# Making the S5 tables during the up projection of the MLP ahead, with the first quarter's fills in its down projection, and silu written to PSUM

## The reference

```
for i in range(DEPTH):
    h = rms_norm(x, norm_mix[i])
    y = [dsa_mixer, rwkv7_mixer, s5_mixer][i % 3](h, ...)
    x = x + y
    x = x + conv_ffn(rms_norm(x, norm_ffn[i]), ...)

def conv_ffn(h, w_up, conv_w, conv_b, w_down):
    u = h @ w_up                        # 1024 -> 2 * 2816
    u = causal_conv_3(u) + conv_b       # one filter of 3 taps per channel
    gate, val = split(u, 2)
    return (silu(gate) * val) @ w_down  # 2816 -> 1024

def s5_mixer(h, a_re, a_im, log_step, b_re, b_im, c_re, c_im, ...):
    step = exp(log_step)
    lam = a_re + 1j * a_im
    lam_bar = exp(lam * step)
    b_bar = (lam_bar - 1) / lam * b
    # 64 groups of 16 channels, state of 64 complex numbers each:
    # state = lam_bar * state + b_bar u ;  y = real(c state) + d h ; gelu ; GLU
```

## Time and profile before

| | |
|---|---|
| median of three runs | 1615.17 us |
| profiled execution, whole | 1617.21 us |
| its span, first to last instruction | 1615.5 us |
| PE busy | 1480.8 us, 92% |
| DVE busy | 1032.3 us, 64% |
| ACT busy | 749.6 us, 46% |
| POOL busy | 618.9 us, 38% |
| chain that ended last | PE 74%, DVE 18%, ACT 4%, issue 2%, POOL 1% |

### The profile page before, as it was taken

One profiled execution on the slowest core, in us unless ns is written; L12 is line 12 of the kernel. 1 busy time (PEld: TensorE's weight loads), 2 busy tenths in 40 slices (PEclk: granted clock), 3 DMA queues, 4 the chain that ended last, 5 costly groups with the idle time before them and its releaser, 6 DMA issues.

```text
span 1615.5 us, 33199 instructions
## 1 busy us (share of the span) xinstructions
PE 1480.8 (92%) x14000; PEld 1382.5 (86%) x14000; DVE 1032.3 (64%) x1572; ACT 749.6 (46%) x1186; POOL 618.9 (38%) x300
## 2 busy tenths in 40 slices
PE   7989999999998884999998546999999998999998
PEld 7888999988787773999987546999999988999998
DVE  4695476735584458467688996467752498367752
ACT  4466465531342332365552212556554457456543
POOL 5322366740010010287652001446754232346763
PEclk9999999999999995999999778999999999999999
DMA  5533355552442001365553001545555343445553
GB/s 156 169 119 105 119 178 187 179 184 93 130 134 77 4 4 51 105 181 186 176 172 122 1 1 54 183 131 183 182 189 169 125 132 105 131 130 181 184 185 103
DMA packets 212054, 210.12 MB, mean 130 GB/s; under 512 B 12098, under 2 KB 211058, under 8 KB 211922
## 3 DMA queue, kind: packets, MB, share of 16 engines
q1 hardware_dynamic: 210784, 206.65, 39.8%
q0 software_dynamic: 800, 1.46, 0.5%
q10 hardware_dynamic: 338, 0.10, 0.0%
HBM read 207.15 MB, written 1.05 MB: 129 GB/s over the span
## 4 chain that ended last, share of the span: by engine, by line
PE 74%; DVE 18%; ACT 4%; issue 2%; POOL 1%; ACTq 0%; DMA 0%; DVEq 0%; POOLq 0%
PE psum L379 16%; PE psum L381 15%; PE psum L380 15%; PE psum L663 7%; PE psum L473 5%; DVE work L2225 4%; PE psum L665 3%; DVE w_low L362 3%; ACT w_high L354 2%; PE psum L410 1%; DVE work L1126 1%; PE psum L1492 1%; PE psum L1506 1%; PE psum L403 1%; DVE work L1931 1%
## 5 line engine op out<-in xcount | busy, mean ns | idle before, releaser
L362 POOL TENSOR_TENSOR w_low<-ring,w_high 128x1024 fp32r<-128x1024 f32 (+1 forms) x184 | 509.6, 2770 | 869.4 <-ACT w_high L354 825.0
L379 PE MATMUL psum<-x_high,w_high 128*128 128x256 f32 x2048 | 589.4, 288 | 28.2 <-issue 16.0
L380 PE MATMUL psum<-x_low,w_high 128*128 128x256 f32 x2048 | 583.6, 285 | 0.0
L381 PE MATMUL psum<-x_high,w_low 128*128 128x256 f32 x2048 | 583.5, 285 | 0.0
L354 ACT ACTIVATE w_high<-ring 128x1024 fp32r<-128x1024 f32 (+1 forms) x368 | 361.7, 1034 | 261.3 <-PE psum L381 159.9
L379 PEld LDWEIGHTS psum<-x_high,w_high 128*128 128x128 f32 x2048 | 397.0, 194 | 34.8 <-issue 20.5
L380 PEld LDWEIGHTS psum<-x_low,w_high 128*128 128x128 f32 x2048 | 397.3, 194 | 1.0 <-issue 1.0
L381 PEld LDWEIGHTS psum<-x_high,w_low 128*128 128x128 f32 x2048 | 397.2, 194 | 0.0
L362 DVE TENSOR_TENSOR w_low<-ring,w_high 128x1024 fp32r<-128x1024 f32 (+1 forms) x184 | 250.8, 1364 | 173.6 <-ACT w_high L354 173.1
L749 DVE SCALAR_TENSOR_TENSOR work<-psum,par,work 128x255 f32<-128x255 f32 (+1 forms) x352 | 145.5, 476 | 147.6 <-ACT work L688 147.5
L663 PE MATMUL psum<-inner,w_high 128*128 128x512 f32 x528 | 186.4, 398 | 2.6 <-DVE w_low L362 2.6
(11 more groups left out here) (303 smaller groups left out, 1874.6 us busy)
## 6 DMA issues: line engine op xcount, KB each, us to landing
ring<-in_ffn_w_up_dram SPq DMA_DIRECT2D x88, 1024.0 KB, 5.1
ring<-in_ffn_w_down_dram SPq DMA_DIRECT2D x32, 1024.0 KB, 5.0
ring<-in_dsa_w_in_dram SPq DMA_DIRECT2D x28, 1024.0 KB, 5.2
ring<-in_ffn_w_down_dram SPq DMA_DIRECT2D x16, 768.0 KB, 4.3
ring<-in_rwkv_w_rkv_dram SPq DMA_DIRECT2D x12, 1024.0 KB, 5.1
ring<-in_dsa_w_out_dram SPq DMA_DIRECT2D x8, 1024.0 KB, 5.1
ring<-in_s_w_glu_dram SPq DMA_DIRECT2D x8, 1024.0 KB, 5.7
ring<-in_rwkv_w_out_dram SPq DMA_DIRECT2D x4, 1024.0 KB, 5.1
```

Of the source, the lines that this page charges most:

```text
L362: eng.tensor_tensor(low, raw, high.bitcast(F32), ALU.subtract).then_inc(sem("w_split", b), 1)
L379: pe.matmul(out_, lhs[0], rhs[0], start=start, stop=False, skip_group_check=True)
L380: pe.matmul(out_, lhs[0], rhs[1], start=False, stop=False, skip_group_check=True)
L381: return pe.matmul(out_, lhs[1], rhs[0], start=False, stop=stop, skip_group_check=True)
```

## The change

- The S5 tables: in the MLP of layer 1, PE transposes `a` after pair 1 and `c` after pair 3. ACT does its two parts after pairs 4 and 5. DVE does table part 0 after pair 4, parts 1 and 2 after pair 6, 3 and 4 after pair 7, 5 and 6 after pair 8, 7 and 8 after pair 9, 9 and 10 after pair 10, and part 11 in step 0 of the down projection.
- The fills of quarter 0 (12 instructions of 1024 elements a row) are made in steps 1, 3, 5 and 7 of that down projection, three in each. `s5_dve` begins with quarter 1.
- The loop over the pairs is written out for this MLP.
- FB and GC are put in other slots of the work area, and the squares of the norm ahead of S5 go where `hT` will be.
- In all four MLPs, silu is written to the PSUM bank of the gate tile, and the product of gate and value reads it there. That bank is free for PE when the product is made, where before it was free when the taps were.

```diff
@@ over_up_tiles
+            if before_s5(L):
+                for j in range(UP_TILES // 2):
+                    pair(j, 0)
+                return
@@
+        TURN_A, TURN_C = 1, 3
+        TABLE_PARTS = {4: (0,), 6: (1, 2), 7: (3, 4), 8: (5, 6), 9: (7, 8), 10: (9, 10)}
+        STEP_PARTS = {0: (11,)}
+        EARLY_FILLS = (1, 3, 5, 7)
@@ freed
-                freed[(L, "up", 2 * j)] = (("taps_done", L), 4 * j + 2)
+                freed[(L, "up", 2 * j)] = (("gated_done", L), j + 1)
@@ add_down
-                        s5_tables(dve, 3 * m + g)
+                        for part in STEP_PARTS.get(3 * m + g, ()):
+                            s5_tables(dve, part)
+                        if 3 * m + g in EARLY_FILLS:
+                            s5_fill(dve, 0, EARLY_FILLS.index(3 * m + g))
@@ mlp_pe
-                if before_s5(L) and j == UP_TILES // 2 - 2:
+                if before_s5(L) and j == TURN_A:
                     s5_turn_a(pe)
-                if before_s5(L) and j == UP_TILES // 2 - 1:
+                if before_s5(L) and j == TURN_C:
                     s5_turn_c(pe)
@@ mlp_act
-                act.activation(conv[:, j % 3, 0], conv[:, j % 3, 0], ACT.Silu).then_inc(sem("silu_done"), 1)
+                act.activation(bank_of((L, "up", 2 * j))[:, :].rearrange("p (c t) -> p c t", c=2), conv[:, j % 3, 0],
+                               ACT.Silu).then_inc(sem("silu_done"), 1)
                 if j:
                     round_inner(j - 1, r)
+                if before_s5(L) and j in (TURN_C + 1, TURN_C + 2):
+                    s5_exponentials(act, j - TURN_C - 1)
@@ mlp_dve
-                dve.tensor_tensor(gated[:, j % 3], conv[:, j % 3, 0], conv[:, j % 3, 1],
-                                  ALU.mult).then_inc(sem("gated_done"), 1)
+                dve.tensor_tensor(gated[:, j % 3], bank_of((L, "up", 2 * j))[:, :].rearrange("p (c t) -> p c t", c=2),
+                                  conv[:, j % 3, 1], ALU.mult).then_inc(sem("gated_done"), 1)
+                if before_s5(L):
+                    for part in TABLE_PARTS.get(j, ()):
+                        s5_tables(dve, part)
@@ s5_fill (a quarter's FB is half 0 and 1, its GC half 2 and 3)
+            if part == 0:
+                step.mark(dve.tensor_tensor(out_, re, x, ALU.mult))
+                tt(t, im, y, ALU.mult)
+                tt(out_, out_, t, ALU.subtract)
+                return
+            tt(out_, re, y, ALU.mult)
+            tt(t, im, x, ALU.mult)
...
@@ s5_dve
-            for q in range(4):
-                fill(FB, b_raw, q, FB_RE, FB_IM, "fb_done")
-                if q:
-                    turned_in(q - 1)
-                    scan(q - 1)
-                    toeplitz(2 * q - 2)
-                    toeplitz(2 * q - 1)
-                fill(GC, c_raw, q, GC_RE, GC_IM, "gc_done")
+            for q in range(1, 4):
+                s5_fill(dve, q, 0)
+                s5_fill(dve, q, 1)
+                turned_in(q - 1)
+                scan(q - 1)
+                toeplitz(2 * q - 2)
+                toeplitz(2 * q - 1)
+                s5_fill(dve, q, 2)
+                s5_fill(dve, q, 3)
```

More of the change, by code:

```diff
@@ L270, in trunk, with squares_of @@
         sq = [slot_view(8, DC, T), slot_view(13, DC, T)]
+        def squares_of(n):
+            return hT if n % 2 == 0 and layers[n // 2] % 3 == 2 else sq[n % 2]
         def updates(L, ffn=0):
@@ L599, in trunk, with over_up_tiles @@
             "p (j c t) -> p j c t", j=3, c=2)
-        def over_up_tiles(eng, pair):
+        def over_up_tiles(eng, pair, L):
+            if before_s5(L):
+                for j in range(UP_TILES // 2):
+                    pair(j, 0)
+                return
             for j in range(ROUND // 2):
@@ L627, in pair @@
                         done, offset = signal(name)
-                        pe.wait_ge(done, r * (4 * PJ) + (value + offset))
+                        pe.wait_ge(done, r * (PJ if name[0] == "gated_done" else 4 * PJ) + (value + offset))
                     else:
@@ L640, in pair @@
                     mm.then_inc(sem("bank_full", bank), 1)
-                if before_s5(L) and j == UP_TILES // 2 - 2:
+                if before_s5(L) and j == TURN_A:
                     s5_turn_a(pe)
-                if before_s5(L) and j == UP_TILES // 2 - 1:
+                if before_s5(L) and j == TURN_C:
                     s5_turn_c(pe)
-            over_up_tiles(pe, pair)
+            over_up_tiles(pe, pair, L)
             for m in range(4):
@@ L721, in pair @@
                     s5_load(pool, L + 1, j)
-            over_up_tiles(pool, pair)
+            over_up_tiles(pool, pair, L)
             rest_of_inner(UP_TILES // 2 - 1, 0)
@@ L730, in pair @@
             def pair(j, r):
-                if before_s5(L) and j == UP_TILES // 2 - 1:
+                if before_s5(L) and j == TURN_A + 1:
                     dve.wait_ge(sem("params_turned"), 1)
@@ L1955, in trunk @@
         QG = S5_Q * GW
-        FB, GC = (flat[:, i * 8192:(i + 1) * 8192].rearrange("p (q r g z) -> p q r g z", q=4, r=2, z=GW) for i in (0, 1))
+        FB, GC = ([work[:, i, :].rearrange("p (r g z) -> p r g z", r=2, z=GW) for i in slots]
+                  for slots in ((7, 1, 2, 3), (8, 5, 6, 0)))
         TZ = FB
         h_tok = work[:, 9, :].rearrange("p (h g s c) -> p h g s c", h=2, s=S5_L, c=S5_C)
-        y_tok = work[:, 8, :].rearrange("p (h s g c) -> p h s g c", h=2, s=S5_L, c=S5_C)
+        y_tok = work[:, 4, :].rearrange("p (h s g c) -> p h s g c", h=2, s=S5_L, c=S5_C)
         u_all = work[:, 10, :].rearrange("p (q h g n) -> p q h g n", q=4, h=2, n=S5_N)
@@ L1968, in trunk @@
         fill_tmp = work[:, 14, 1024:2048]
-        with_cos, with_sin = (work[:, 8, i * 512:(i + 1) * 512].rearrange("p (r z) -> p r z", r=2) for i in (0, 1))
+        with_cos, with_sin = (work[:, 4, i * 512:(i + 1) * 512].rearrange("p (r z) -> p r z", r=2) for i in (0, 1))
         decay8 = work[:, 15, 0:1024].rearrange("p (q z) -> p q z", q=4)
@@ L2321, in s5_tables, with s5_fill @@
                 double(2 ** (part - 7))
+        def s5_fill(dve, q, half):
+            step = vector_step
+            then, tt, ts, complex_product = s5_math(dve)
+            kind, part = half // 2, half % 2
+            dst, raw, c_re, c_im, signal_ = ((FB, b_raw, FB_RE, FB_IM, "fb_done"), (GC, c_raw, GC_RE, GC_IM, "gc_done"))[kind]
+            g = slice(q * S5_Q, (q + 1) * S5_Q)
+            shape = [P, S5_Q, S5_L, S5_C]
+            re, im = (raw[:, v, g].unsqueeze(2).to_broadcast(shape) for v in (0, 1))
+            x, y = (coef[:, v, :, g].rearrange("p k g -> p g k").unsqueeze(3).to_broadcast(shape) for v in (c_re, c_im))
+            out_ = dst[q][:, part].rearrange("p g (k c) -> p g k c", k=S5_L)
+            t = fill_tmp.rearrange("p (g k c) -> p g k c", g=S5_Q, k=S5_L)
+            if q == 0 and part == 0:
+                dve.wait_ge(*((sem("s5_in", 2), 16 * S5_DMAS[2]), (sem("c_ready"), 2))[kind])
+            if part == 0:
[5 more added lines that the diff above has]
+            tt(t, im, x, ALU.mult)
+            if dst is GC:
+                ins = dve.scalar_tensor_tensor(out=out_, in0=out_, scalar=-1.0, in1=t, op0=ALU.mult, op1=ALU.subtract)
+            else:
+                ins = dve.tensor_tensor(out_, out_, t, ALU.add)
+            ins.then_inc(sem(signal_), 1)
+            dve.wait_ge(sem(signal_), q + 1)
         def s5_dve(dve, L):
@@ L2325, in s5_dve @@
             then, tt, ts, complex_product = s5_math(dve)
-            def fill(dst, raw, q, c_re, c_im, signal_):
-                g = slice(q * S5_Q, (q + 1) * S5_Q)
-                shape = [P, S5_Q, S5_L, S5_C]
-                re, im = (raw[:, v, g].unsqueeze(2).to_broadcast(shape) for v in (0, 1))
-                x, y = (coef[:, v, :, g].rearrange("p k g -> p g k").unsqueeze(3).to_broadcast(shape) for v in (c_re, c_im))
-                out_ = [dst[:, q, v].rearrange("p g (k c) -> p g k c", k=S5_L) for v in (0, 1)]
-                t = fill_tmp.rearrange("p (g k c) -> p g k c", g=S5_Q, k=S5_L)
-                step.mark(dve.tensor_tensor(out_[0], re, x, ALU.mult))
-                tt(t, im, y, ALU.mult)
-                step.mark(dve.tensor_tensor(out_[0], out_[0], t, ALU.subtract))
-                tt(out_[1], re, y, ALU.mult)
-                tt(t, im, x, ALU.mult)
-                if dst is GC:
-                    ins = dve.scalar_tensor_tensor(out=out_[1], in0=out_[1], scalar=-1.0, in1=t, op0=ALU.mult,
-                                                   op1=ALU.subtract)
-                else:
-                    ins = dve.tensor_tensor(out_[1], out_[1], t, ALU.add)
-                ins.then_inc(sem(signal_), 1)
-                dve.wait_ge(sem(signal_), q + 1)
             def toeplitz(k):
@@ L2352, in toeplitz @@
                 dve.wait_ge(sem("lag_full"), k + 1)
-                dve.tensor_tensor(TZ[:, q, :, g0:g0 + 4], psum[:, at:at + 2, :].rearrange("p h (g z) -> p h g z", g=4),
```

(1 more changed line is left out.)

22 lines of the change are left out of this document (9 added, 13 removed).

## The result

The changed kernel takes 1630.2 us (median of 8 runs, 1628.31 to 1637.83). The kernel before took 1617.6 us beside it (8 runs). The ratio is 1.0083, 95% interval [1.0058, 1.0107]: slower by 13.4 us in the means (the medians differ by 12.6). The forecast was 12.0 us slower. The profiled execution took 1630.4 us, forecast 1629.2, and its span is 1628.6 us, at a mean granted clock of 0.958.

What follows compares the result with a forecast made beforehand. PE bounds the up projections; layer 1's down projection adds 5.6 us of waits for DVE's weight split. +1.9 + 2.7 + 22.6 + 1.6 - 5.6 - 3.5 - 7.7 = +12.0 us, giving 1627.2 us; range 1608 to 1634.

Steps and rivals of the forecast that it cites:

- Silu through PSUM: All MLPs: the product takes about 0.7 instead of 2.9 us of DVE per pair, by itself worth nothing in layers 0, 2, 3.
- rival 4: All MLPs: the product reading PSUM is still blocked by POOL, 1635 us; chance 0.03.
- Turning `a`: Layer 1's up projection, after pair 1: PE waits for the last load of `a`, +1.9 us (0 to 3).
- Exponentials: Layer 1's up projection: ACT rounds weights late, PE waits 1.4 us before tile 12, 1.3 before tile 14; +2.7 us.
- Tables: Layer 1's up projection from tile 16 and first down steps: PE waits for DVE's weight split, +22.6 us by queue walk.
- rival 3: Layer 1's MLP: long waits drop TensorE's clock to 1.2 GHz from 2.4, +5 us, 1632 us; chance 0.10.
- Exclusion as the mechanism: Layer 1's MLP: a DVE instruction with two SBUF operands and a POOL instruction exclude each other; 3.7 us of tables cost 6.5.
- Rivals 1 and 2: Layer 1's MLP: tables hide, 1598.7 us, chance 0.14; or taps always fall beside POOL, 1610 to 1615, chance 0.14.
- the ledger's bounds: Pair 6 to down step 3, layer 1: summed DVE and POOL work makes PE late by 13.0 to 29.3 us.
- Fills: Layer 1's down projection: fills in steps 1, 3, 5, 7 cost one more wait, +1.6 us at step 10 (0 to 3).
- Norm tail: Behind layer 1's down projection: the norm's reciprocal follows at 6.4 us instead of 9.8, -3.5 us.
- S5: Start of S5: quarter 0's fills go, -14.6 us, but DVE waits 6.8 us for the states; gain -7.7 us.

Runs made afterwards that it cites:

- e1: The kernel before with only silu written to PSUM and the product reading it there, in all four MLPs; ratio to the kernel before 1.0009.
- e5: The changed kernel with the two transposes of `a` at tile 2 of layer 1's up projection instead of tile 1; ratio to the kernel before 1.0074.
- e4: The changed kernel with one operand of most table instructions in PSUM and 16 small copies added; 1621.0 us, ratio to the kernel before 1.0020.
- e7: The changed kernel with the edits of e4, e5 and e6 together; 1615.2 us, ratio to the kernel before 0.9977.
- e3: The changed kernel with quarter 0's 12 fills back at the start of S5, tables left in the up projection; 1637.0 us, ratio to the kernel before 1.0117.
- e6: The changed kernel with quarter 1's two GC fills moved ahead of the first `turned_in` in S5; 1628.3 us, ratio to the kernel before 1.0066.

## Why the prediction was right, step by step

- **Silu through PSUM, worth nothing alone:** right (e1). The product takes 0.684 us, forecast 0.7; rival 4 is out.
- **Turning `a`, +1.9:** the wait is 1.79 us. Without it PE was 1.7 us earlier up to tile 20 (e5), and the waits between stayed as they were, so the term stands. In the time of the whole it could not be told from nothing.
- **Exponentials, +1.4 and +1.3:** measured 1.49 and 1.27.
- **Tables, 22.6 us of waits:** 4.2, 0.7 and 3.4 at tiles 16, 18 and 20 were 3.76, none and 3.84. The first steps of the down projection were to wait 6.5, 2.2 and 5.7; they waited 0.91 at the first and 6.90 at the third. The term measured 15.4 us, 7.2 less than forecast. The slow clock, which the sum put at nothing and rival 3 at +5 on top, took 6.3. That the two nearly cancel is why the sum came out, and in part it is luck. The prediction's own argument, that a slower PE is partly hidden because DVE is late, would make it more than luck, but it did not hold where the runs can test it. Behind the wait ahead of tile 16 (2.48 and 2.49 us) e4 ran for 4.89 us at a mean granted clock of 0.65 and e7 at 1.00, with the same code. Ahead of tile 18 both waited equally long, the first row being e4 and the second e7:

```profile
788.75 0.35 PE L383 MATMUL psum<-x_high,w_high 128*128 128x256 f32 x1 [0.90 <-DVE w_low L366]
```
```profile
788.00 0.35 PE L383 MATMUL psum<-x_high,w_high 128*128 128x256 f32 x1 [0.90 <-DVE w_low L366]
```

  From the end of the one wait to the end of the other e4 took 14.14 us and e7 12.65: the slow clock cost 1.5 us on top. Whether it shortened waits elsewhere, in the down projection above all, was not isolated.
- **Exclusion as the mechanism:** shown by e4, which adds instructions and wins 10 us. Rivals 1 and 2 are out, since the up projection took 143 us. That the walk through the queues was a better price than the middle of the ledger's bounds is not shown: waits and slow clock together, 21.7 us, lie no farther from that middle, 21.2, than from the walk's 22.6.
- **Fills, +1.6 in the MLP:** the wait at step 10 is 1.76 us, and goes in e3.
- **Norm tail, -3.5:** -3.2.
- **S5, -7.7 with 6.8 us of DVE waiting:** -6.1 with 5.74. The first `turned_in` came 8.8 us nearer to the reciprocal; 2.7 us of that were given back later in S5, within what S5 of the same code differs by (169.8 and 172.8 in before and e1). The sign named for a right forecast, S5 8 to 11 us shorter, was not met; nor was the one of 14 us of waits in the first steps of the down projection, which were 7.8.

In all, the MLP with its norm was forecast at 1.9 + 2.7 + 22.6 + 1.6 - 5.6 - 3.5 = +19.7 and came to +18.9, S5 at -7.7 and came to -6.1. So close an agreement is partly chance: the same MLP code took 228.8 us in e6, which would have been +21.5.

## What to carry to other kernels

Before small vector work is moved under a phase in which POOL streams, look at where its operands lie: here a 32-element operation with both in SBUF lasted as long as the POOL instruction beside it, and one operand in PSUM freed it, even at the price of extra copies. A freed engine is worth time only where something waits for it. Where an edit seems to bring less than the wait that it removes, compare the stretch with a second profile of the same code first: the pattern of waits that seemed to eat up the gain of e5 was there without the edit, in e6. Where such work must be laid under matmuls, spread it by the slack of each tile and each step: the same instructions, moved by one or two steps, were worth 4 to 5 us here.
